# A TensorE-bound encoder kernel: the weights' parts are written at another offset inside their ring slots

## The reference

```
x = x + diff_attention(rmsnorm(x))   # x @ attn_w_in (2048 x 8192), scores, softmax, @ attn_w_out (2048 x 2048)
x = x + conformer_conv(rmsnorm(x))   # x @ conv_w_in (2048 x 6144), 31-tap depthwise convolution,
                                     # layer norm, silu gate, @ conv_w_out (2048 x 2048)
return rmsnorm(x)
```

## Time and profile before

| | us |
|---|---|
| median of 3 runs | 851.54 |
| the profiled execution's own time | 851.34 |
| span of its trace | 849.6 |
| PE busy | 840.9 (99%) |
| VectorE (DVE) busy | 646.5 (76%) |
| ScalarE (ACT) busy | 449.2 |
| GpSimd (POOL) busy | 225.9 |

### The profile page before, as it was taken

How to read it: one execution, slowest core, us unless ns; L and a number is a source line. 1 busy time by engine, 2 the same in 40 slices (tenths; PEclk the granted TensorE clock), 3 DMA queues, 4 the chain that set the end, 5 groups by cost and what they waited for, 6 DMA issues and landing times.

```text
span 849.6 us, 13845 instructions
## 1 busy us (share of the span) xinstructions
PE 840.9 (99%) x5628; PEld 769.2 (91%) x5628; DVE 646.5 (76%) x1097; ACT 449.2 (53%) x589; POOL 225.9 (27%) x107
## 2 busy tenths in 40 slices
PE   9999999999999999999999999999999999999996
PEld 9988899889988899888888899999999999988885
DVE  7569684697658684698788978999999997566651
ACT  7746543546336543556544365454554556594432
POOL 0200000000000000002000008888888887680000
PEclk9999999999999999999999999999999999999999
DMA  9976565535654566534655565556555555549502
GB/s 329 395 283 242 168 204 198 182 130 198 206 189 148 167 195 203 184 113 160 231 182 184 185 210 184 174 177 199 182 179 187 194 178 179 195 150 344 196 3 99
DMA packets 99649, 163.68 MB, mean 193 GB/s; under 512 B 3584, under 2 KB 40704, under 8 KB 99080
## 3 DMA queue, kind: packets, MB, share of 16 engines
q1 hardware_dynamic: 98112, 160.64, 56.3%
q10 hardware_dynamic: 1480, 2.25, 0.7%
HBM read 160.76 MB, written 3.69 MB: 194 GB/s over the span
## 4 chain that ended last, share of the span: by engine, by line
PE 96%; DMA 1%; SPq 1%; DVE 1%; ACT 1%; issue 0%; ACTq 0%
PE ps_acc L1215 17%; PE ps_acc L1218 17%; PE ps_acc L1217 17%; PE ps_acc L1204 14%; PE ps_acc L1201 14%; PE ps_acc L1203 14%; DMA sb_w_raw<-in_attn_w_in 1%; PE ps_a L1306 0%; PE ps_a L1305 0%; PE ps_d L1292 0%; PE ps_d L1291 0%; PE ps_a L1304 0%; PE ps_d L1290 0%; PE ps_a L1178 0%; SPq L327 0%; SPq L328 0%
## 5 line engine op out<-in xcount | busy, mean ns | idle before, releaser
L446 ACT ACTIVATE sb_w_hi<-sb_w_raw 128x2048 fp32r<-128x2048 f32 x140 | 267.1, 1914 | 252.9 <-PE ps_acc L1218 171.4
L418 POOL TENSOR_TENSOR sb_w_lo<-sb_w_raw,sb_w_hi 128x2048 fp32r<-128x2048 f32 x45 | 208.5, 4639 | 409.5 <-ACT sb_w_hi L446 409.5
L788 DVE TENSOR_TENSOR sb_w_lo<-sb_w_raw,sb_w_hi 128x2048 fp32r<-128x2048 f32 x95 | 216.1, 2289 | 103.9 <-ACT sb_w_hi L446 103.5
L1215 PE MATMUL ps_acc<-sb_conv_hi,sb_w_hi 128*128 128x256 f32 x768 | 215.0, 280 | 0.0
L1218 PE MATMUL ps_acc<-sb_conv_hi,sb_w_lo 128*128 128x256 f32 x768 | 213.8, 278 | 0.0
L1217 PE MATMUL ps_acc<-sb_conv_lo,sb_w_hi 128*128 128x256 f32 x768 | 213.7, 278 | 0.0
L1020 DVE SCALAR_TENSOR_TENSOR ps_d<-sb_uT,sb_dwT,ps_d 128x256 f32<-128x256 f32 x480 | 188.9, 480 | 4.5 <-ACT ps_d L670 4.5
L1201 PE MATMUL ps_acc<-sb_w_hi,sb_act_hi 128*128 128x512 f32 x384 | 151.4, 394 | 0.0
L1203 PE MATMUL ps_acc<-sb_w_lo,sb_act_hi 128*128 128x512 f32 x384 | 151.3, 394 | 0.0
L1204 PE MATMUL ps_acc<-sb_w_hi,sb_act_lo 128*128 128x512 f32 x384 | 151.3, 394 | 0.0
L1218 PEld LDWEIGHTS ps_acc<-sb_conv_hi,sb_w_lo 128*128 128x128 f32 x768 | 144.2, 188 | 0.0
(11 more groups left out here) (168 smaller groups left out, 875.1 us busy)
## 6 DMA issues: line engine op xcount, KB each, us to landing
sb_w_raw<-in_attn_w_in SPq DMA_DIRECT2D x60, 1024.0 KB, 5.7
sb_w_raw<-in_conv_w_in SPq DMA_DIRECT2D x64, 512.0 KB, 4.6
sb_w_raw<-in_attn_w_out SPq DMA_DIRECT2D x16, 1024.0 KB, 5.0
sb_w_raw<-in_conv_w_in SPq DMA_DIRECT2D x16, 1024.0 KB, 5.1
sb_w_raw<-in_conv_w_out SPq DMA_DIRECT2D x16, 1024.0 KB, 5.0
sb_w_raw<-in_attn_w_in SPq DMA_DIRECT2D x16, 256.0 KB, 4.6
sb_xs<-in_x SPq DMA_DIRECT2D x2, 1024.0 KB, 13.8
sb_x_in<-in_x_turned SPq DMA_DIRECT2D x15, 128.0 KB, 4.4
```

The costliest lines, as they stand in the source:

```text
L418: pool.tensor_tensor(w_lo[c % RING][:], w_raw[c % RING][:], w_hi[c % RING][:].bitcast(F32), ALU.subtract).then_inc(lo_ready_pool, 1)
L446: act.activation(w_hi[slot][:], w_raw[slot][:], ACT.Copy).then_inc(hi_ready, 1)
L788: dve.tensor_tensor(w_lo[slot][:], w_raw[slot][:], w_hi[slot][:].bitcast(F32), ALU.subtract).then_inc(lo_ready, 1)
L1215: pe.matmul(into, left_hi, hi[:, kt], start=(kt == 0 and f % 2 == 0), stop=False, skip_group_check=True)
```

## The change

The slots of `w_hi` and `w_lo` get 128 elements (512 bytes) more than a chunk needs, and each chunk's parts are written and read at an offset within the slot. A function `place(c)` gives the offset in elements of four bytes by the chunk's number: 12 for the first pair of heads; for the later pairs 8 in the turned groups (4 in the k group of the last pair) and 84 (80 in the last pair) in the groups by rows; 48 for the attention output; 96, 124, 116, 100, 92 and 84 for the six stretches of eight chunks of the convolution input; 32 for the last product. `w_raw` and the DMAs into it are unchanged.

The added 4,096 bytes in a partition come from the scratch room of dynamic DMAs, which is set to 8,192 bytes instead of 16,384. In the built program `w_hi` then begins at byte 57,472, its slots follow at 8,704 bytes, and `act_hi`, `conv_hi` and the others keep 192 modulo 512.

The instructions on every engine are the same as before in number, kind, shape, waits and order; no row of PE's 4,843, nor of any other engine's, moves. Only addresses in them differ. So no order is shown.

```diff
+W_GAP = 128
+HEAD_AT, HEAD_ROWS_AT = 12, 12
+PAIR_AT, PAIR_ROWS_AT = 8, 84
+LAST_AT, LAST_ROWS_AT = 4, 80
+OUT_AT = 48
+CONV_AT = (96, 124, 116, 100, 92, 84)
+CONV_OUT_AT = 32
-        w_hi = [sb(f"w_hi{i}", [P, CK, GW], F32R) for i in range(RING)]
-        w_lo = [sb(f"w_lo{i}", [P, CK, GW], F32R) for i in range(RING)]
+        w_hi = [sb(f"w_hi{i}", [P, CK * GW + W_GAP], F32R) for i in range(RING)]
+        w_lo = [sb(f"w_lo{i}", [P, CK * GW + W_GAP], F32R) for i in range(RING)]
...
+        def place(c):
+            if c >= CHUNKS_CONV:
+                return CONV_OUT_AT
+            if c >= CHUNKS_OUT:
+                return CONV_AT[(c - CHUNKS_OUT) // (2 * NCH)]
+            if c >= CHUNKS_ATT:
+                return OUT_AT
+            j, t = c // 16, c % 16 // NCH
+            if t == 0 and j:
+                return PAIR_AT
+            head, pair, last = (HEAD_AT, PAIR_AT, LAST_AT) if t < 2 else (HEAD_ROWS_AT, PAIR_ROWS_AT, LAST_ROWS_AT)
+            return head if j == 0 else last if j == PAIRS - 1 else pair
...
+        def w_part(parts, c):
+            at = place(c)
+            return parts[c % RING][:, at:at + CK * GW].rearrange("p (k n) -> p k n", k=CK)
...
-                pool.tensor_tensor(w_lo[c % RING][:], w_raw[c % RING][:], w_hi[c % RING][:].bitcast(F32),
+                pool.tensor_tensor(w_part(w_lo, c), w_raw[c % RING][:], w_part(w_hi, c).bitcast(F32),
                                    ALU.subtract).then_inc(lo_ready_pool, 1)
...
-                act.activation(w_hi[slot][:], w_raw[slot][:], ACT.Copy).then_inc(hi_ready, 1)
+                act.activation(w_part(w_hi, c if like is None else like), w_raw[slot][:], ACT.Copy
+                               ).then_inc(hi_ready, 1)
...
+                high, low = w_part(w_hi, c), w_part(w_lo, c)
...
-                        pe.matmul(into, left_hi, w_hi[i][:, k], start=(kt == 0 and not filled), stop=False,
+                        pe.matmul(into, left_hi, high[:, k], start=(kt == 0 and not filled), stop=False,
...
-                    left_hi, left_lo = w_hi[i][:, k, f * P:(f + 1) * P], w_lo[i][:, k, f * P:(f + 1) * P]
+                    left_hi, left_lo = (w_part(part, c)[:, k, f * P:(f + 1) * P] for part in (w_hi, w_lo))
...
-    nc = bacc.Bacc("TRN2", target_bir_lowering=False, num_devices=1)
+    nc = bacc.Bacc("TRN2", target_bir_lowering=False, num_devices=1, dynamic_dma_scratch_size=8192)
```

More of the change, by code:

```diff
@@ L292, in by_pool, with pair_chunk @@
             return c == POOL_SEAM or POOL_FROM <= c < POOL_TO
+        def place(c):
[10 more added lines that the diff above has]
+            return head if j == 0 else last if j == PAIRS - 1 else pair
+        def pair_chunk(j, i):
+            in_loop = type(j) is not int
+            return 16 * (1 if in_loop else j) + i
+        def w_part(parts, c):
+            at = place(c)
+            return parts[c % RING][:, at:at + CK * GW].rearrange("p (k n) -> p k n", k=CK)
         def low_part_ready(eng, c):
@@ L442, in _, with high_part @@
         def _(act):
-            def high_part(c, slot, loads):
+            def high_part(c, slot, loads, like=None):
                 act.wait_ge(landed[slot], 16 * loads)
                 act.wait_ge(w_free, c + 1)
-                act.activation(w_hi[slot][:], w_raw[slot][:], ACT.Copy).then_inc(hi_ready, 1)
+                act.activation(w_part(w_hi, c if like is None else like), w_raw[slot][:], ACT.Copy
+                               ).then_inc(hi_ready, 1)
             def load_table(func):
@@ L468, in _ @@
                     act.wait_ge(piece_landed(p), 16)
-                    act.activation(w_hi[slot][:, rows], w_raw[slot][:, rows], ACT.Copy
+                    act.activation(w_part(w_hi, slot)[:, rows], w_raw[slot][:, rows], ACT.Copy
                                    ).then_inc(hi_ready if closes else head_hi, 1)
@@ L509, in pair_slot @@
                 if i in (9, 10):
-                    high_part(16 * j + i + RING, i % NCH, 4 * j + i // NCH + 2)
+                    high_part(16 * j + i + RING, i % NCH, 4 * j + i // NCH + 2, pair_chunk(j, i + RING))
                     for hq in ((0, 1) if i == 9 else (2, 3)):
@@ L784, in link, with low_part @@
                 dve.wait_ge(dve_done, chain["base"] + chain["n"])
-            def low_part(c, slot):
+            def low_part(c, slot, like=None):
+                like = c if like is None else like
                 dve.wait_ge(hi_ready, c + 1)
-                dve.tensor_tensor(w_lo[slot][:], w_raw[slot][:], w_hi[slot][:].bitcast(F32), ALU.subtract
+                dve.tensor_tensor(w_part(w_lo, like), w_raw[slot][:], w_part(w_hi, like).bitcast(F32), ALU.subtract
                                   ).then_inc(lo_ready, 1)
@@ L806, in _ @@
                     dve.wait_ge(piece_landed(0), 16)
-                    dve.tensor_copy(w_hi[slot][:, rows], w_raw[slot][:, rows]).then_inc(first_hi, 1)
+                    dve.tensor_copy(w_part(w_hi, slot)[:, rows], w_raw[slot][:, rows]).then_inc(first_hi, 1)
                 dve.wait_ge(x_landed[p], 16)
@@ L819, in _ @@
                     dve.wait_ge(head_hi, pieces_left_open(p))
-                dve.tensor_tensor(w_lo[slot][:, rows], w_raw[slot][:, rows], w_hi[slot][:, rows].bitcast(F32),
-                                  ALU.subtract).then_inc(lo_ready if closes else head_lo, 1)
+                dve.tensor_tensor(w_part(w_lo, slot)[:, rows], w_raw[slot][:, rows],
+                                  w_part(w_hi, slot)[:, rows].bitcast(F32), ALU.subtract).then_inc(lo_ready if closes else head_lo, 1)
                 if p == LAM_AT:
@@ L1190, in lambda_sums, with project @@
                 pe.matmul(bank_a[0][:, 0:2], ones[:], lam_prod, start=True, stop=True).then_inc(a_full, 1)
-            def project(i, par, hi, lo, halfway=None, tiles=range(ST), done=w_free, filled=False):
+            def project(c, i, par, hi, lo, halfway=None, tiles=range(ST), done=w_free, filled=False):
+                high, low = w_part(w_hi, c), w_part(w_lo, c)
                 for k in range(CK):
@@ L1200, in project @@
                         left_hi, left_lo = hi[:, kt, st * P:(st + 1) * P], lo[:, kt, st * P:(st + 1) * P]
-                        pe.matmul(into, left_hi, w_hi[i][:, k], start=(kt == 0 and not filled), stop=False,
+                        pe.matmul(into, left_hi, high[:, k], start=(kt == 0 and not filled), stop=False,
                                   skip_group_check=filled)
-                        pe.matmul(into, left_hi, w_lo[i][:, k], start=False, stop=False, skip_group_check=filled)
-                        ins = pe.matmul(into, left_lo, w_hi[i][:, k], start=False, stop=(kt == KT - 1),
+                        pe.matmul(into, left_hi, low[:, k], start=False, stop=False, skip_group_check=filled)
+                        ins = pe.matmul(into, left_lo, high[:, k], start=False, stop=(kt == KT - 1),
                                         skip_group_check=filled)
@@ L1220, in project_tile, with project_turned @@
                 return ins
[L1222 removed]
+            def project_turned(c, i, par, hi, lo):
                 for kt in range(i * CK, (i + 1) * CK):
[L1225 removed]
+                    ins = project_tile(c, par, hi, lo, kt)
                 ins.then_inc(w_free, 1)
@@ L1247, in head_slot @@
                     into = [acc[:, f // 2, (f % 2) * SEQ:(f % 2 + 1) * SEQ] for f in range(GW // P)]
-                    left = [[part[i][:, kt % CK, f * P:(f + 1) * P] for f in range(GW // P)] for part in (w_hi, w_lo)]
+                    left = [[w_part(part, i)[:, kt % CK, f * P:(f + 1) * P] for f in range(GW // P)] for part in (w_hi, w_lo)]
                     pe.wait_ge(split_hi, kt + 1)
```

16 lines of the change are left out of this document (8 added, 8 removed).

## The result

The changed kernel takes 853.38 us (median of 22 runs, 852.45 to 854.69), the kernel before 851.61 us (22 runs). The ratio is 1.0016, with a 95% interval of 1.0009 to 1.0022: slower by 0.16%, where 837.8 us was forecast. The profiled execution has a span of 851.8 us, 2.2 us more than the span of before.

What follows compares the result with a forecast made beforehand. PE's own matmul stream bounds the kernel. From the profiled 851.3 us, 13.7 us for turned chunks, with 0 for rows and other engines, gives 837.6, or 837.8 us with the median 0.2 us higher; range 817 to 852 us.

Steps and rivals of the forecast that it cites:

- What bounds the kernel: Whole kernel: PE busy 840.9 of 849.6 us, nothing else late; only the distance between matmul starts can pay or cost.
- ScalarE, VectorE, GpSimd, scratch room: 0: Engines writing and reading the weight parts, and dynamic DMA room: slight changes stay covered by the ring's lead; 0 us.
- I choose 113.3 ns: Turned chunks in attention and convolution: 62 slower ones go from 117.9 to 113.3 ns per matmul, gaining 13.7 us.
- The upper bound: Turned chunks: if all go to the scores' 120 ns, loss 6.2 + 4.5 = 10.7 us, 4.5 in 14 fast chunks.
- Rows: 0: The 64 chunks by rows: no second pace seen at 233 ns, so 0; ends 24.6 us gain, 10.8 us loss.
- a rival for a gain: Chunks by rows: they also speed up, to 226.7 ns, gaining 9.7 us, total 828.1 us; chance 0.26.
- Slower by nearness: Attention chunks, mainly: operands starting closer modulo 512 bytes run slower, costing 2.8 and 1.3 us, total 855.6 us; chance 0.13.
- Reshuffled: Convolution: new offsets merely redraw which stretches are fast; 844.0 to 854.6 us, middle 849 us; chance 0.14.
- VectorE as the next bound: Convolution: VectorE's taps need 5.46 us per chunk, covering PE at 5.44 us but not at 5.23 us.
- The rule in the Trainium skill: All matmuls: TensorE's two read ports are independent, so offsets are worth 0 and the time is 851.5 us.
- The lower bounds of 109 and 217 ns: Best distances from L1350, for turned chunks (29.4 us gain) and chunks by rows (24.6 us gain).
- What would show it: PE's 20 us stretches: right if turned about 179 matmuls, rows 87 or 88; turned wrong at 172 or fewer.

Runs made afterwards that it cites:

- e2_conv_back: Changed kernel with only the convolution input chunks' offsets set back to 0; 847.18 us, ratio 0.9946 to the kernel before.
- the last run: Kernel before with rows at offset 80, turned chunks at 32 but 29 in the second chunk behind each break; 832.60 us, ratio 0.976.
- the shuffled sweep: Against the kernel before, each chunk at its own offset, all 32 multiples of 4 elements within 512 bytes in shuffled order; 854.81 us, one run.

## Why the prediction was wrong, point by point

- **What bounds the kernel** was right: PE's stream, next to no wait, and only the distance between matmuls can pay.
- **ScalarE, VectorE, GpSimd, scratch room: 0** was right. L477, L821 and L449 take 1.92, 2.29 and 4.62 us, against the earlier trace rows, and the layout alone gives a ratio of 0.9998.
- **"I choose 113.3 ns, since it is the only other pace that this very stream has shown"** is the step that failed. It took the two paces as the only two, and the offset as something that picks between them. In fact each relative address has one, two or three paces of its own, 340 to 370 per three turned matmuls, and at nine of the sixteen distances of the table none is under 353. That 113.3 ns can be had in the slow chunks was right: with offset 32 and rows at 0, 61 of the 76 turned chunks have it. The nine offsets of the turned chunks gave 350 (a gain of 0.85 + 0.43 us), 360 (loss 0.3) and, in the convolution, 350 to 360 with chunks 80 to 87 left at 353. The step's 13.7 us became a loss of 3.3 us (0.30 - 0.85 - 0.43 + 4.31). The trace had the warning: the scores showed a third pace at a second address, so there was no reason to expect only two.
- **What that choice overlooked in the baseline:** 14 chunks were already at the fast pace, and an address that cannot have it loses 0.2 to 0.3 us in each. Of the 4.3 us lost in the convolution 3.4 us lie in these 14 chunks (at 355 or 356 instead of 340). The upper bound counted this loss (4.5 us), the forecast did not.
- **Rows: 0**, with a rival for a gain. Measured -1.3 us: 680 in the last pair (the rival's 226.7 ns exactly), about 695 in the middle ones, 710 in the first, none in 32 of 64 chunks. The rival was right that a pace of 226.7 ns exists; the offsets chosen hit it in 8 chunks. Its reason, that the offsets move furthest there, misreads the change: the last product moves by 32, and the turned chunks of the convolution move by 84 to 124.
- **"Slower by nearness"** had the right sign for the first pair only: 12 elements gave 360 and 710, 0.9 us, and some of these chunks had 352 and 680 in another execution at the same offset (e2_conv_back). But 32 and 48 bytes of distance gave 350, faster than the 353 at 64 bytes. It is not nearness that decides, but the exact distance modulo 256 bytes, with the way in.
- **"Reshuffled"** came nearest in the convolution: it priced the loss of the 14 fast chunks at 3.1 us, and they lost 3.4. But the places are no new draws at the old paces: the layout alone kept every chunk's pace, and new offsets brought new paces. Both theories turned out true in part. The address limits which paces there are, and where several are possible the way in decides (the offset before and, at the start of a stream, something that varies from execution to execution). With offset 32 that is worth 5.8 us of turned chunks between two kernels that differ only in the offset of the rows.
- **VectorE as the next bound at 5.46 us per chunk** was right as far as the last run goes: with PE at 5.44 us VectorE is busy all the time and PE does not yet wait at the transposes. The first wait on VectorE came where the prediction did not look, in the first pair.
- **The rule in the Trainium skill**: "SBUF — State Buffer" of the Trainium skill, section "Who interferes with whom", gives TensorE two independent read ports and says that TensorE never waits on anyone. By it all offsets are worth nothing. Here the same instructions with the same operands' sizes took 340 to 370 and 680 to 720 ns by the distance of their operands and the way in. The measurements decide: relative addresses count. Whether it is the reads that wait, no run shows.
- **The lower bounds of 109 and 217 ns** came from L1350, a plain float32 matmul with 256 columns, and no run came down to them: the best are 113.3 and 226.7 ns. So the lower end of the range, 817 us, rested on paces that no run shows; the best kernel takes 832.6 us.
- **Small slips:** the stretch from 682 us on has 178 matmuls, not 179 (its chunks are at 340.0 all the same), and the estimate that is given as 27 us for the chunks by rows is 26 by its own figures. Neither changes the forecast.
- **What would show it**: 172 or fewer in 20 us was named as the sign that the turned step is wrong, and the stretch from 682 us on has 172.

What stays open is the mechanism below this. That a weight load and the matmul before it read at the same time, and get in each other's way where their addresses meet, would fit the dependence on the distance. It was not shown: no run here separates the address of the load from that of the matmul it accompanies, or gives `w_hi` and `w_lo` offsets of their own. Why some distances have two steady paces is open as well.

## What to carry to other kernels

In a stream of matmuls without waits, measure the distance between starts and not the busy time; if it differs between stretches of the same instructions, look at the distance of the two operands' start addresses modulo 256 bytes. It can be swept in one kernel, one offset per chunk, but a pace found there must be confirmed in the final order, because a distance can have two paces and a stretch mostly keeps the one it came in with. When some stretches are fast already, count what a change can take from them before counting what it may bring.

## What the runs showed of the hardware that was not expected

- Float32r matmuls of 256 columns with a weight load each: 113.3 to 123.3 ns apart; with 512 columns 226.7 to about 240 ns, at the full clock all the while. The period in the address is 256 bytes, and single elements (4 bytes) matter.
- No distance gave less than 340 and 680 per three: at 2.4 GHz that is 16 steps over 256 columns and 32 over 512. The plain float32 records of the kernel before, 217 ns apart, are of another kind (256 columns, two records each) and set no floor for these.
- The start varies from trace to trace: the wait of PE for its fifth chunk was 0.6 to 2.8 us, with the DMA engines full behind it (share 1.01 in the stretch from 32 us on). The three longest are 2.0 us (the shuffled sweep) and 2.8 us (32 and 96, 29 and 32 in turn). It may be one of the places where executions of a kernel come to differ by 1 to 3 us, and the wait of 2.2 us in the last trace another. With one trace for each kernel this is not shown.
